# Decay matrices of a state-space mixer: running sums broadcast through DRAM instead of three matmuls a head

## What is computed

```python
dt = jax.nn.softplus(dtb.astype(jnp.float32) + dt_bias.astype(jnp.float32))
a_neg = -jnp.exp(a_log.astype(jnp.float32))
...
acum = jnp.cumsum(dtr * a_neg.reshape(G_B, hg), axis=2)
xdt = xr * dtr[..., None]
seg = acum[:, :, :, None] - acum[:, :, None, :]
decay = jnp.exp(jnp.where(causal, seg, -jnp.inf))
cb = jnp.einsum('bctgn,bcsgn->bctsg', cr, br)
y_diag = jnp.einsum('bctsgh,bcsghp->bctghp', cb[..., None] * decay, xdt)
```

## Time and profile before

| what | value |
|---|---|
| median of 3 runs | 2137.43 us (2135.99 to 2141.94) |
| the profiled execution | 2138.36 us |
| its span, first to last instruction | 2136.4 us |
| TensorE busy | 2069.0 us, 97% |
| VectorE busy | 1390.0 us, 65% |
| ScalarE busy | 1089.2 us, 51% |
| GpSimd busy | 88.0 us, 4% |
| mean granted TensorE clock | 0.989 |

### The profile page before, as it was taken

How to read it: one execution, slowest core, us unless ns; L and a number is a source line. 1 busy time by engine, 2 the same in 40 slices (tenths; PEclk the granted TensorE clock), 3 DMA queues, 4 the chain that set the end, 5 groups by cost and what they waited for, 6 DMA issues and landing times.

```text
span 2136.4 us, 35852 instructions
## 1 busy us (share of the span) xinstructions
PE 2069.0 (97%) x14507; PEld 1886.3 (88%) x14507; DVE 1390.0 (65%) x2044; ACT 1089.2 (51%) x1715; POOL 88.0 (4%) x132
## 2 busy tenths in 40 slices
PE   6999899999999999999989999999999999999998
PEld 4788799889978989989979979997888988988996
DVE  6865778745556676667675556556568666766555
ACT  4577457534343568547444443444458735743442
POOL 0200000000000001200000000000000230000000
PEclk9999999999999999999999999999999999999999
DMA  6433445645744444443635754574443434463563
GB/s 246 158 119 119 168 158 186 227 138 178 258 160 158 139 139 142 135 139 119 217 119 178 252 181 139 185 252 158 158 136 121 158 121 137 138 215 120 185 208 118
DMA packets 271628, 351.55 MB, mean 165 GB/s; under 512 B 9891, under 2 KB 225549, under 8 KB 271501
## 3 DMA queue, kind: packets, MB, share of 16 engines
q1 hardware_dynamic: 271501, 349.75, 48.8%
HBM read 348.68 MB, written 1.05 MB: 164 GB/s over the span
## 4 chain that ended last, share of the span: by engine, by line
PE 87%; DVE 6%; DMA 3%; ACT 2%; issue 1%; SPq 1%; POOL 0%; DVEq 0%; ACTq 0%; POOLq 0%
PE ps L733 26%; PE ps L735 25%; PE ps L734 25%; DVE ring_r L1703 3%; DMA ring<-in_ffn_w_out 1%; PE ps L1144 1%; ACT ring_hi L1272 1%; PE ps L1048 1%; DMA ring<-in_w_mix_out 1%; PE ps L1164 1%; PE ps L921 1%; PE ps L1075 1%; PE ps L1208 1%; DMA ring<-in_w_in 1%; DVE conv_s L2154 0%
## 5 line engine op out<-in xcount | busy, mean ns | idle before, releaser
L1703 DVE TENSOR_TENSOR ring_r<-ring,ring_hi 128x1024 fp32r<-128x1024 f32 x602 | 735.7, 1229 | 464.9 <-ACT ring_hi L1272 464.1
L1272 ACT ACTIVATE ring_hi<-ring 128x1024 fp32r<-128x1024 f32 x602 | 633.4, 1059 | 644.6 <-PE ps L735 615.5
L733 PE MATMUL ps<-xT_hi,ring_hi 128*128 128x256 f32 x2784 | 791.7, 284 | 2.2 <-DVE xT_r L1703 2.2
L734 PE MATMUL ps<-xT_r,ring_hi 128*128 128x256 f32 x2784 | 781.4, 281 | 0.0
L735 PE MATMUL ps<-xT_hi,ring_r 128*128 128x256 f32 x2784 | 781.3, 281 | 0.0
L733 PEld LDWEIGHTS ps<-xT_hi,ring_hi 128*128 128x128 f32 x2784 | 525.7, 189 | 15.5 <-issue 11.0
L734 PEld LDWEIGHTS ps<-xT_r,ring_hi 128*128 128x128 f32 x2784 | 525.7, 189 | 0.1
L735 PEld LDWEIGHTS ps<-xT_hi,ring_r 128*128 128x128 f32 x2784 | 525.5, 189 | 0.0
L735 PE MATMUL ps<-ring_hi,tok_r 128*128 128x512 f32 x472 | 187.1, 396 | 0.0
L734 PE MATMUL ps<-ring_r,wide_r 128*128 128x512 f32 x440 | 173.0, 393 | 0.0
L733 PE MATMUL ps<-ring_hi,wide_r 128*128 128x512 f32 x400 | 159.2, 398 | 3.7 <-DVE ring_r L1703 3.7
(11 more groups left out here) (304 smaller groups left out, 2760.1 us busy)
## 6 DMA issues: line engine op xcount, KB each, us to landing
ring<-in_w_mix_in SPq DMA_DIRECT2D x88, 1024.0 KB, 4.9
ring<-in_ffn_w_in SPq DMA_DIRECT2D x80, 1024.0 KB, 5.0
ring<-in_ffn_w_out SPq DMA_DIRECT2D x44, 1024.0 KB, 4.8
ring<-in_w_branch SPq DMA_DIRECT2D x24, 1024.0 KB, 5.1
ring<-in_w_in SPq DMA_DIRECT2D x22, 1024.0 KB, 5.1
ring<-in_w_ffn_up SPq DMA_DIRECT2D x22, 1024.0 KB, 5.0
ring<-in_w_ffn_down SPq DMA_DIRECT2D x11, 1024.0 KB, 4.8
ring<-in_w_mix_out SPq DMA_DIRECT2D x8, 1024.0 KB, 5.7
```

The lines of the kernel that those rows point to most:

```text
L733: pe.matmul(out_, stat[0], mov[0], start=first, stop=False)
L734: pe.matmul(out_, stat[0], mov[1], start=False, stop=False)
L1272: act.activation(half_of(high_of(s), s, q), half_of(ring[:, s % SLOTS, :], s, q), ACT.Copy).then_inc(w_hi, 1)
L1703: return dve.tensor_tensor(lo, whole, hi.bitcast(F32), ALU.subtract)
```

## The change

GpSimd's `seg_w` and TensorE's sdecay go away. Two steps are new in each layer, ahead of two halves of the last `va` chunk. In cum_rows, TensorE forms the running sum of step times a within each tile of 128 tokens, as rows (a head a row), and for the first tile the sum of what is left to its end. ScalarE copies the rows to `cum_row`, and GpSimd stores them in a new DRAM tensor `decay_rows`. In cum_cols, TensorE transposes the rows to columns, VectorE copies them into `dts`, and GpSimd loads the rows of pairs 0 and 1 back, each broadcast to all 128 partitions of `act_s`.

sdecay(p) is now six GpSimd instructions of 128x128: row minus the token's own sum, held at or under zero, for the two blocks within a tile, and row plus the remainder for the block from the first tile to the second. ScalarE takes Exp in place. Behind its six, GpSimd issues the load of pair p+2. VectorE multiplies by `cbm` alone. The step dt_s is folded into the values: turn_xs is a multiply on VectorE in place of ScalarE's copy. dscore(0) on TensorE waits for cum_done. Line numbers of the changed kernel are larger by 8 (TensorE's first lines) to 24.

```diff
--- before.py
+++ after.py
@@ -274,6 +274,9 @@
+    for name, h in (("cum_rows", 0), ("cum_cols", 1)):
+        steps.insert(steps.index(("half", mix[7], h, 0)), (name,))
     def before(a, b):
@@ -380,12 +383,14 @@
         third_hi = flat(xbc_r[:, 0:KD, :])
-        seg_w = act_s[:, :, 0:3 * P]
         soft4 = tok[:, 0:4 * CAUS].rearrange("p (a n) -> p a n", a=4)
...
             return (ex if u % 4 < 2 else lmat)[:, u % 2, 0:CAUS]
+        rem_of = lambda u: dts[:, 0, u:u + 1]
+        cum_of = lambda u, t: dts[:, 1, t * NH + u:t * NH + u + 1]
@@ -1049,6 +1057,20 @@
+                def cum_rows():
+                    pe.wait_ge(dt_done, L + 1)
+                    for t in range(T):
+                        pe.matmul(ps[0:NH, S0, t * P:(t + 1) * P], dts[:, 4, t * NH:(t + 1) * NH], upto[:, 0:P], start=True, stop=True)
+                    pe.matmul(ps[:, S1, 0:NH], after, dts[:, 4, 0:NH], start=True, stop=True).then_inc(cum_ready, 1)
+                def cum_cols():
+                    pe.wait_ge(cum_copied, L + 1)
+                    for t in range(T):
+                        tr = pe.transpose(ps[:, S1, (2 + t) * NH:(3 + t) * NH], cum_row[:, t * P:(t + 1) * P], ident[0:NH, 0:NH])
+                    tr.then_inc(cum_turned, 1)
                 def turn_qk(j):
@@ -1070,6 +1092,8 @@
                         pe.wait_ge(d_masked, lap(L, u, 2 * DH))
+                    else:
+                        pe.wait_ge(cum_done, L + 1)
                     for m in range(2):
@@ -1151,20 +1175,6 @@
-                def sdecay(p):
-                    pe.wait_ge(seg_built, lap(L, 2 * p + 2, NH))
-                    if p == 0:
-                        pe.wait_ge(cb_masked, lap(L, 2, 2))
-                    else:
-                        pe.wait_ge(seg_exp, lap(L, 2 * p, NH))
-                    for m in range(2):
-                        b = S0 + m
-                        w = seg_w[:, m, :]
-                        pe.matmul(ps[:, b, 0:TOK], w[:, 0:P], upto, start=True, stop=False)
-                        pe.matmul(ps[:, b, P:TOK], w[:, 2 * P:3 * P], upto[:, 0:P], start=False, stop=True)
-                        pe.matmul(ps[:, b, TOK:CAUS], w[:, P:2 * P], upto[:, 0:P], start=True, stop=True).then_inc(seg_ready, 1)
                 def sout(p):
@@ -1188,7 +1198,7 @@
                     if p == 0:
-                        pe.wait_ge(seg_exp, lap(L, NH, NH))
+                        pe.wait_ge(cb_masked, lap(L, 2, 2))
                     else:
@@ -1563,6 +1577,10 @@
+                def cum_rows():
+                    act.wait_ge(cum_ready, L + 1)
+                    act.activation(cum_row[:, :], ps[0:NH, S0, 0:TOK], ACT.Copy).then_inc(cum_copied, 1)
                 def turn_qk(j):
@@ -1602,18 +1620,10 @@
-                def turn_xs(j):
-                    act.wait_ge(xs_turned, lap(L, j + 1, 4))
-                    act.activation(xs[:, :, 2 * j * P:(2 * j + 2) * P], tiles(TB + j % 2), ACT.Copy).then_inc(xs_copied, 1)
                 def sdecay(p):
                     for u in (2 * p, 2 * p + 1):
-                        act.wait_ge(seg_ready, lap(L, u + 1, NH))
-                        if u < 2:
-                            act.wait_ge(d_turned, lap(L, 2 * DH, 2 * DH))
-                        elif u >= 4 and u % 2 == 0:
-                            act.wait_ge(y_ready, lap(L, p - 1, NH // 2))
-                        act.activation(decay_of(u), ps[:, S0 + u % 2, 0:CAUS], ACT.Exp).then_inc(seg_exp, 1)
+                        act.wait_ge(seg_built, lap(L, u + 1, NH))
+                        act.activation(decay_of(u), decay_of(u), ACT.Exp).then_inc(seg_exp, 1)
@@ -2225,6 +2237,18 @@
+                def cum_cols():
+                    dve.wait_ge(cum_turned, L + 1)
+                    dve.tensor_copy(dts[:, 0, 0:NH], ps[:, S1, 0:NH])
+                    dve.tensor_copy(dts[:, 1, :], ps[:, S1, 2 * NH:4 * NH]).then_inc(cum_done, 1)
+                def turn_xs(j):
+                    dve.wait_ge(xs_turned, lap(L, j + 1, 4))
+                    i, o = (a.rearrange("p t (h d) -> p t h d", d=HD) for a in (tiles(TB + j % 2), xs[:, :, 2 * j * P:(2 * j + 2) * P]))
+                    step_ = dts[:, 2, :].rearrange("p (t h) -> p t h", t=T)[:, :, 4 * j:4 * j + 4]
+                    dve.tensor_tensor(o, i, step_.unsqueeze(3).to_broadcast([P, T, 4, HD]), ALU.mult).then_inc(xs_copied, 1)
                 def turn_qk(j):
@@ -2287,12 +2311,8 @@
                         dve.wait_ge(seg_exp, lap(L, u + 1, NH))
-                        g = u // (NH // 2)
                         e = decay_of(u)
-                        for t, r in enumerate((slice(0, TOK), slice(TOK, CAUS))):
-                            ins_ = dve.scalar_tensor_tensor(e[:, r], e[:, r], dts[:, 2, t * NH + u:t * NH + u + 1],
-                                                            cbm[:, g, r], ALU.mult, ALU.mult)
-                        ins_.then_inc(l_ready, 1)
+                        dve.tensor_tensor(e, e, cbm[:, u // (NH // 2), :], ALU.mult).then_inc(l_ready, 1)
@@ -2388,22 +2410,50 @@
+                def load_decay(p):
+                    pool.dma_start(act_s[:, p % 2, :], decay_rows[L:L + 1, 2 * p:2 * p + 2, :].rearrange("l h n -> l (h n)").to_broadcast([P, 2 * TOK]))\
+                        .then_inc(decay_loaded[p % 2], 16)
+                def cum_rows():
+                    pool.wait_ge(cum_copied, L + 1)
+                    pool.dma_start(decay_rows[L], cum_row[:, :]).then_inc(row_stored, 16)
+                def cum_cols():
+                    pool.wait_ge(row_stored, 16 * (L + 1))
+                    pool.wait_ge(xbc_done, lap(L, 6, 6))
+                    for p in range(2):
+                        load_decay(p)
                 def sdecay(p):
...
                     if p == 0:
-                        pool.wait_ge(dt_done, lap(L, 1, 1))
-                        pool.wait_ge(xbc_done, lap(L, 6, 6))
-                    for u in (2 * p, 2 * p + 1):
-                        if p:
-                            pool.wait_ge(seg_ready, lap(L, u - 1, NH))
-                        for n, (m, t) in enumerate(((after, 0), (after, 1), (ones, 1))):
-                            ins_ = pool.tensor_tensor(seg_w[:, u % 2, n * P:(n + 1) * P], m,
-                                                      dts[:, 4, t * NH + u:t * NH + u + 1].to_broadcast([P, P]), ALU.mult)
-                        ins_.then_inc(seg_built, 1)
+                        pool.wait_ge(cum_done, L + 1)
+                        pool.wait_ge(d_turned, lap(L, 2 * DH, 2 * DH))
+                    elif p == 1:
+                        pool.wait_ge(oa_turned, lap(L, 4, 4))
+                    else:
+                        pool.wait_ge(y_ready, lap(L, p - 1, NH // 2))
+                    pool.wait_ge(decay_loaded[p % 2], 16 * (NH // 4 * L + p // 2 + 1))
+                    for m in range(2):
+                        u = 2 * p + m
+                        e, row = decay_of(u), act_s[:, p % 2, m * TOK:(m + 1) * TOK]
+                        pool.tensor_scalar(e[:, 0:P], row[:, 0:P], cum_of(u, 0), 0.0, ALU.subtract, ALU.min)
+                        pool.tensor_scalar(e[:, P:TOK], row[:, P:TOK], rem_of(u), None, ALU.add)
+                        pool.tensor_scalar(e[:, TOK:CAUS], row[:, P:TOK], cum_of(u, 1), 0.0, ALU.subtract, ALU.min).then_inc(seg_built, 1)
+                    if p + 2 < NH // 2:
+                        pool.wait_ge(seg_built, lap(L, 2 * p + 2, NH))
+                        load_decay(p + 2)
...
                         sdecay(step[1])
+                    elif step[0] == "cum_rows":
+                        cum_rows()
+                    elif step[0] == "cum_cols":
+                        cum_cols()
                     elif step[0] == "dnorm":
@@ -2433,5 +2483,6 @@
     out = nc.dram_tensor("out", (1, TOK, D), F32, kind="ExternalOutput").ap()
-    program(nc, aps, out)
+    decay_rows = nc.dram_tensor("decay_rows", (LAYERS, NH, TOK), F32, kind="Internal").ap()
+    program(nc, aps, out, decay_rows)
     return run_bass_kernel_spmd(nc, [arrays], core_ids=[0]).results[0]["out"]
```

19 lines of the change are left out of this document (15 added, 4 removed).

## The result

The changed kernel takes **2112.43 us** (median of 4 runs, 2111.42 to 2114.48); the kernel before took 2137.55 beside it. The ratio is 0.9882, with an interval of 0.9870 to 0.9895: 25.1 us less. The forecast was 2112, in a range of 2107 to 2124.

The account below looks back on a forecast made before the run. TensorE, busy 97% of the span, was taken as the bound. 2138.4 - 28.4 + 0.8 + 1.8 = 2112.6, against the median 2111.6; it predicted 2112 us, with an 8 in 10 range of 2107 to 2124.

Parts of the forecast that it names:

- The term that carries it, -28.4 us: Decay stage on TensorE: removing three fp32 matmuls a head saves 14.20 us a layer, 28.4 in both.
- The running sums, +0.8: TensorE in cum_rows and cum_cols: added matmuls and transposes cost 0.4 us a layer, 0.8 in all.
- cum_rows fills the hole and stands 0.07 us over it: Three new TensorE matmuls, 0.66 us, go into a 0.59 us hole where a product waits for drained banks.
- The wait for the value tiles, +1.8: TensorE's transposes wait for turn_xs's multiplies in VectorE's queue: 0.9 us a layer, 1.8 in all.
- fit in 7.0: Decay stage: GpSimd's six products, 2.71 to 6.13 us, fit in the 7.0 us before ScalarE asks for them.
- Has six again, with other operands: GpSimd in sdecay: six 128x128 products a pair as before, taken at the old rows' 2.71 to 6.13 us.
- Rival B: GpSimd becomes the bound: six of 1.0 and an issue of 2 us, period 8.0, 2131 us; chance 0.11.
- no more than the old did: GpSimd's new products, which read SBUF too, wait for VectorE as the old did, and no more.
- rival C: Broadcasts land late, a wait in place of the matmuls: an 18 us landing gives 2156 us; chance 0.05.
- 10.6 us put: Broadcast load p+2, issued behind pair p's six products, has 10.6 us to land; landing taken as 5 us, hidden.
- rival A: Granted clock drops again at the new matmuls: 5 us lost a layer, 2122 us; chance 0.06.
- Rival D: Weight stream (DMA, ScalarE's and VectorE's splits) holds TensorE at the old pace, no gain: 2137 us; chance 0.03.

Follow-up runs that it names:

- run 2: Changed kernel with six fp32 matmuls a pair of heads put back on TensorE, into banks nobody reads: 2140.64 us, ratio 1.0012.
- run 3: Changed kernel with turn_xs's first two multiplies put ahead of the weight split on VectorE: 2111.09 us, ratio 0.9872.
- Runs 4 and 5: Changed kernel with more 128x128 GpSimd instructions into an unread buffer: one more a head (4) 2120.25 us, ratio 0.9919; three more (5) 2150.26 us, ratio 1.0067.
- Run 6: Changed kernel without the broadcast loads of pairs 2 to 7, which take the rows of pairs 0 and 1: 2112.96 us, ratio 0.9889.
- run 7: Changed kernel with each broadcast issued one pair ahead instead of two: 2124.23 us, ratio 0.9943.

## Why the prediction was right

**The term that carries it, -28.4 us.** Right: 13.98 us a layer measured against 14.20, and run 2 gives 13.9 back when the matmuls alone return. TensorE was busy in every part of the stage, and is so after. Each term was off a little: by the table +0.4 us here, +0.7 for the running sums and -0.9 for the value tiles, both layers together. These nearly cancel. That the forecast came within 0.5 us, and not within 1 or 2, is luck.

**The running sums, +0.8.** 0.73 a layer against 0.4. The step that failed is "cum_rows fills the hole and stands 0.07 us over it": the three matmuls and the next product take the hole and 0.32. The two transposes of cum_cols cost 0.41, where 0.20 and a part of 0.1 for the change of kind were put. TensorE's rows at both places:

```profile
739.79 0.40 PE L743 MATMUL ps<-ring_hi,xT_r 128*128 128x512 f32 x1
740.12 0.28 PE L1064 MATMUL ps<-const,dts 128*16 128x128 f32 x1
...
740.66 0.40 PE L1065 MATMUL ps<-dts,const 128*128 128x16 f32 x2
740.90 0.48 PE L741 MATMUL ps<-ring_hi,xT_hi 128*128 128x512 f32 x1
...
748.45 0.29 PE L1071 MATMUL ps<-const,cum_row 16*128 16x16 f32 x2
748.67 0.50 PE L741 MATMUL ps<-ring_hi,xT_hi 128*128 128x512 f32 x1
```

At the first place the new matmuls start 0.33 us behind a product, where the next product would start after 0.23, and the three take 0.78 (740.12 to 740.90) where 0.66 was put. At the second the two new transposes start 0.96 us behind the start of the other eight (747.49), where eight take 0.79 alone, and take 0.22. The first product behind each place starts the next one 0.33 and 0.34 us later and not 0.23, but that was nearly so before (0.30, 740.47 to 740.77; 0.32, 747.81 to 748.13). So the price of a few small matmuls is in the seams ahead of them, where one kind of product follows another: 0.10 and 0.17 us.

**The wait for the value tiles, +1.8.** 0.6 a layer against 0.9 (run 3). The place and the engine were as foreseen: the multiplies behind one split. VectorE had the first ready at 846.2 and the second at 846.8, 0.5 to 0.6 later than put. But the whole place had moved: TensorE reached the first transposes 0.87 us later than before, and VectorE the products of dnorm 0.90 later. Against each other they were 0.3 us closer than put.

**GpSimd: covered, but mis-sized.** The forecast took 2.71 to 6.13 us for six and judged both to fit in 7.0. Measured are 5.5 to 7.4 in the last six pairs of both layers, 6.3 on average (871.37 to 878.35; 879.28 to 885.15; 901.55 to 907.91), and 7 of these 12 pairs are past the upper bound. "Has six again, with other operands", priced with the old rows, is the step that failed. The new form is slower alone, 4.0 us for six against 2.2, and it meets longer VectorE instructions. The prediction also set the loop against the period of 6.65 us and left out GpSimd's own: with the issue of a load it is 7.2, more than 6.65. What kept the sum right was not foreseen, and is luck: the two distances of 9.4 us raise the mean to 7.46, the 7.0 held by tenths of a microsecond, and behind it stood TensorE's cover, of which 3.8 us remain at the pair shown. Runs 4 and 5 show how near it was: with eight instructions a pair GpSimd sets the pace. Rival B's mechanism was the true danger; its period of 8.0 would be reached by 0.8 us more a pair. Its price was too high, though. The period of 9.0 in run 4 cost 7 us, where 8.0 was to cost 19, since the loss counts against 7.46 and the cover comes first. Its issue of 2 us stands in no run: the issue took 0.60 us and the wait ahead of it 0.30.
The Trainium skill (SBUF — State Buffer, Practical consequences) says that VectorE with two inputs in SBUF and GpSimd, when it reads SBUF, shut each other out for a whole instruction. The rows at 865.79 and 866.19 of the kernel before, where the two go by turns, agree with it, and so does the row at 905.00 for GpSimd (1.63 us beside a split that started before it, 0.70 alone). At 902.63 GpSimd's row starts first, and still it is GpSimd's that is long (1.75 us), while the split of 902.71 keeps its 1.21. The "no more than the old did" that the prediction drew from that rule was wrong: beside VectorE the old six took 0.5 us more than alone, the new ones 2.3.

**The broadcasts: hidden, rival C out.** Their landing is in the changed kernel's list of DMA issues (KB each, median us to landing):

```profile
act_s<-decay_rows POOLq DMA_DIRECT2D x16, 256.0 KB, 3.9
...
decay_rows<-cum_row POOLq DMA_DIRECT2D x2, 16.0 KB, 1.8
```

3.9 us (3.4 to 5.9) against the 5 taken. The room was less than the 10.6 us put, since the six ahead of a load take longer: from the issue to the first instruction that needs it are 7.0 to 9.4 us at the last four loads of the first layer (900.91 to 907.90 the shortest). Run 6 shows the loads free and run 7 what they cost with half the lead. The Trainium skill (DMA: Bandwidth & Descriptors, Anatomy of one DMA — SWDGE (gpsimd) path) gave an estimate of 2.6 us; the measured 3.9 decides, half again as long.

**The clock: rival A out.** PEclk is 1.00 from 740 to 744, around the new matmuls, and 1.00 in the decay stage, and the mean over the span 0.987 against 0.989. **Rival D** fell with the result, since it had the time stay at 2137. VectorE's two products of a pair took 1.02 to 1.19 us against the 1.1 put.

## What to carry to other kernels

When one engine is busy all through a stage, what is taken from it is gained at full length, provided that nothing else arrives too late; here that sum held to 2%. Add the seams of what is put elsewhere on it, here 0.1 to 0.2 us each. Price a moved step anew on the engine that gets it, by the form of the instruction and by how long the neighbour engine's instructions beside it are, and not by the count of instructions. Set each engine's own period against the loop's, mean and shortest. Write down the cover twice, for the next engine in the chain and for the bound, and afterwards add one dummy instruction where it is thinnest: a step that is free may be one instruction away from setting the pace.
